# The MLP down projection in seven half-size products per unit, and two norms in one chain

## The reference, cut to what matters

```python
D_MODEL, SEQ, DEPTH, D_FF = 1024, 256, 2, 4096

def rmsnorm(x, g):
    y = x * lax.rsqrt(jnp.mean(x * x, axis=-1, keepdims=True) + EPS)
    return y * g

def squared_relu_mlp(h, w_up, w_down):
    return jnp.square(jax.nn.relu(h @ w_up)) @ w_down

def first_block(x, mem, ...):
    h = x
    for layer in range(DEPTH):
        h = h + mixer(rmsnorm(h, ...), ...)
        h = h + memory_cross_attention(rmsnorm(h, xa_norm[layer]), mem, ...)
        h = h + squared_relu_mlp(rmsnorm(h, mlp_norm[layer]), mlp_w_up[layer], mlp_w_down[layer])
    return rmsnorm(h, final_norm)

def second_block(x, c, ...):
    sh1, sc1, gt1, sh2, sc2, gt2 = split(silu(c) @ w_ada + b_ada)
    h = rmsnorm(x, norm1_w) * (1.0 + sc1) + sh1
    x = x + gt1 * hybrid_mixer(h, ...)
    h2 = rmsnorm(x, norm2_w) * (1.0 + sc2) + sh2
    return x + gt2 * expert_choice_ffn(h2, ...)
```

## Time and profile before

| | us |
|---|---|
| median of 3 runs | 1802.83 |
| lowest, highest | 1796.73, 1804.12 |
| profiled execution | 1800.43 |
| its span | 1798.6 |
| mean granted clock in it | 0.939 |
| TensorE busy, share of the span | 1567.6, 87% |
| VectorE busy | 450.9, 25% |
| ScalarE busy | 258.8, 14% |
| DMA, mean over the span | 220 GB/s |

### The profile page before, as it was taken

One profiled execution on the slowest core, in us unless ns is written; L12 is line 12 of the kernel. 1 busy time (PEld: TensorE's weight loads), 2 busy tenths in 40 slices (PEclk: granted clock), 3 DMA queues, 4 the chain that ended last, 5 costly groups with the idle time before them and its releaser, 6 DMA issues.

```text
span 1798.6 us, 20532 instructions
## 1 busy us (share of the span) xinstructions
PE 1567.6 (87%) x9012; PEld 1163.4 (65%) x9012; DVE 450.9 (25%) x1056; ACT 258.8 (14%) x606; POOL 30.3 (2%) x52
## 2 busy tenths in 40 slices
PE   5999999999999999999999899999977656566665
PEld 4867688888886777888888788768863212121212
DVE  3633015330033420253200355652330000000000
ACT  1232021000011510210000222232021000000000
POOL 0000000000010000000000002000000000000000
PEclk9999999999999999999999899998989888887778
DMA  9425316664443054157644101342549999999997
GB/s 383 148 93 187 140 47 234 240 266 154 153 158 140 1 187 152 47 222 272 250 166 143 47 1 48 117 134 102 246 175 388 429 429 429 429 430 429 429 428 316
DMA packets 42824, 395.25 MB, mean 220 GB/s; under 512 B 15856, under 2 KB 18288, under 8 KB 19056
## 3 DMA queue, kind: packets, MB, share of 16 engines
q1 hardware_dynamic: 42032, 392.46, 55.3%
q0 software_dynamic: 272, 1.05, 0.2%
q10 hardware_dynamic: 432, 0.44, 0.1%
HBM read 391.31 MB, written 2.62 MB: 219 GB/s over the span
## 4 chain that ended last, share of the span: by engine, by line
PE 74%; DMA 22%; DVE 2%; issue 1%; ACT 1%; ACTq 0%; DVEq 0%
PE pb L433 66%; DMA ring<-in_w_experts 22%; PE pb L521 6%; DMA small_w<-in_small_w 1%; PE pb L582 1%; PE pb L642 0%; DVE rstd L1616 0%; ACT arena L1274 0%; PE pb L1101 0%; PE pb L961 0%; PE pb L1108 0%; DVE xT L2152 0%; DVE arena L1676 0%; PE pb L727 0%; DVE sml L1703 0%
## 5 line engine op out<-in xcount | busy, mean ns | idle before, releaser
L433 PE MATMUL pb<-hT,ring 128*128 128x256 f32 x2176 | 483.2, 382 | 0.0
L433 PEld LDWEIGHTS pb<-hT,ring 128*128 128x128 f32 x2176 | 412.5, 191 | 62.9 <-issue 7.8
L433 PE MATMUL pb<-arena,ring 128*128 128x256 f32 (+3 forms) x1344 | 250.1, 353 | 3.1 <-DVE xT L1846 1.5
L433 PEld LDWEIGHTS pb<-arena,ring 128*128 128x128 f32 (+2 forms) x1344 | 219.5, 183 | 32.9 <-issue 5.0
L1274 ACT ACTIVATE arena<-pb 128x512 f32<-128x512 f32 (+4 forms) x166 | 77.9, 480 | 522.0 <-PE pb L433 429.8
L433 PE MATMUL pb<-ring,hT 128*32 128x512 f32 (+2 forms) x512 | 94.0, 657 | 36.9 <-DMA ring<-in_w_experts 36.9
L433 PE MATMUL pb<-arena 128*64 128x128 f32 (+5 forms) x592 | 96.7, 457 | 29.5 <-DMA arena<-in_w_experts 17.0
L521 PE MATMUL pb<-arena,ring 128*128 128x256 f32 x512 | 118.2, 382 | 0.0
L2140 DVE SCALAR_TENSOR_TENSOR side<-side,pb 128x256 f32<-128x256 f32 x16 | 6.7, 422 | 410.5 <-ACT side L1274 410.5
L521 PEld LDWEIGHTS pb<-arena,ring 128*128 128x128 f32 x512 | 94.9, 190 | 14.6 <-issue 2.9
L433 PE MATMUL pb<-ring,arena 128*32 128x512 f32 (+1 forms) x416 | 63.8, 720 | 45.4 <-DMA ring<-in_w_experts 45.4
(11 more groups left out here) (254 smaller groups left out, 1204.1 us busy)
## 6 DMA issues: line engine op xcount, KB each, us to landing
ring<-in_w_dense SPq DMA_DIRECT2D x86, 2048.0 KB, 8.0
ring<-in_w_experts SPq DMA_DIRECT2D x72, 2048.0 KB, 36.1
arena<-in_w_experts SPq DMA_DIRECT2D x24, 2048.0 KB, 36.0
ring<-in_w_dense SPq DMA_DIRECT2D x2, 1536.0 KB, 7.5
cons<-in_cons SPq DMA_DIRECT2D x1, 1808.0 KB, 19.6
xT<-in_xT SPq DMA_DIRECT2D x1, 1024.0 KB, 6.3
side<-in_memT POOLq DMA_DIRECT2D x1, 1024.0 KB, 6.3
out<-xT SPq DMA_DIRECT2D x4, 256.0 KB, 2.2
```

Of the source, the lines that this page charges most:

```text
L433: return nc.tensor.matmul(o, l, r, start=st, stop=sp)
```

## The change

Each unit of the down projection is a product of a 256x1024 block of hidden values and a 1024x512 block of weights. It is cut in halves along all three dimensions and computed as 7 products of half the size instead of 8, in Strassen's way. Four sums of weight quarters and four sums of hidden quarters are made by VectorE (`prepare`): three of the former go into spare memory and one in place into the ring slot; the latter go into `hT`. Now a chunk of 128 tokens is the stationary operand and 256 output features are the moving one. The 7 products collect over the four units of a side in the halves of four banks, 0 to 3 for side 0 and 4 to 7 for side 1. `collect` on VectorE, after a copy on ScalarE, makes the four quarters of the result from them; these have tokens on partitions, so TensorE transposes them (16 transposes per layer, 8 of them after unit 5 for side 0, and 8 after unit 7 for side 1) before VectorE adds them to `xT`.

The final norm and the next block's norm are made in one chain. ScalarE squares each chunk of `xT` twice, plain and scaled by `final_norm`; VectorE sums both over the chunks 0 to 6 (`add_both`); TensorE makes both means with 6 matmuls, the second with a term that accounts for EPS; VectorE scales `xT` directly into `hT` with the product of both gains (`gg`), and only then makes the final norm's `xT`.

The slots, sizes of loads and their order don't change. GpSimd waits for `pads` before it clears its workspace, whose memory the sums use. The core of the diff:

```diff
+        wsum = [view(arena, 10240, 4, S), view(arena, 11264, 4, S), view(arena, 12288, 3, S)]
+        hsum = [view(hTt, 512 * i, 4, P) for i in range(4)]
+        quarters = [more[:, S * i:S * (i + 1)] for i in range(4)]
...
-                for side_ in range(2):
-                    names = [f"dn{layer}_{side_}_{f}" for f in range(4)]
-                    banks = [fill(nm, f) for f, nm in enumerate(names)]
-                    for g in range(4):
-                        w, u = take()
+                for i in range(8):
+                    side_, g = divmod(i, 4)
+                    if g == 0:
+                        pq = [fill(f"pq{layer}_{side_}_{j}", 4 * side_ + j) for j in range(4)]
+                    w, u = take()
+                    down_unit[layer, i] = u
+                    h = hid[:, 8 * g:8 * g + 8, :]
+                    rows_ = {"11": lambda k: h[:, k, TOK[0]], "12": lambda k: h[:, 4 + k, TOK[0]], "22": lambda k: h[:, 4 + k, TOK[1]]}
+                    rows_ |= {f"s{j + 1}": lambda k, j=j: hsum[j][:, k, :] for j in range(4)}
+                    cols_ = {"11": lambda k: w[:, k, FEAT[0]], "21": lambda k: w[:, 4 + k, FEAT[0]], "22": lambda k: w[:, 4 + k, FEAT[1]],
+                             "t1": lambda k: wsum[0][:, k, :], "t2": lambda k: wsum[1][:, k, :], "t3": lambda k: w[:, k, FEAT[1]],
+                             "t4": wide_sum}
+                    step = 8 * (8 * layer + i)
+                    for n, (j, l, r, needs) in enumerate((((0, 0), "11", "11", 0), ((0, 1), "12", "21", 0), ((1, 1), "s1", "t1", 2),
+                                                          ((2, 0), "s2", "t2", 4), ((1, 0), "22", "t4", 5), ((2, 1), "s3", "t3", 7),
+                                                          ((3, 0), "s4", "22", 8))):
+                        if needs:
+                            pe.wait_ge(ws_ready, step + needs)
+                        for k in range(4):
+                            if side_ == 0 and n < 2 and k % 2 == 0:
+                                pe.wait_ge(hid_ready, 16 * layer + 4 * g + 2 * n + k // 2 + 1)
+                            last = nc.tensor.matmul(pq[j[0]][:, FEAT[j[1]]], rows_[l](k), cols_[r](k),
+                                                    start=g == 0 and k == 0 and n in (0, 2, 3, 6), stop=g == 3 and k == 3,
+                                                    skip_group_check=True)
+                        if n >= 2 or (n == 1 and g == 3):
+                            mark(last, f"pq{layer}_{side_}_{j[0]}", g == 3, u if n == 6 else None)
+                            product_done[layer, i, n] = (pq_bank := fillings[f"pq{layer}_{side_}_{j[0]}"][0], marks[pq_bank])
+                    if i == 0:
+                        modulation(6 * layer + 5)
+                    if i in (5, 7):
                         for f in range(4):
-                            for k in range(DC):
-                                if side_ == 0 and f == 0 and k % 2 == 0:
-                                    pe.wait_ge(hid_ready, 16 * layer + 4 * g + k // 2 + 1)
-                                last = mm(banks[f][:, 0:S], w[:, k, f * P:(f + 1) * P],
-                                          hid[:, 8 * g + k, :], g == 0 and k == 0, g == 3 and k == DC - 1)
-                            if g == 3 or f == 3:
-                                mark(last, names[f], g == 3, u if f == 3 else None)
-                        if side_ == 0 and g == 0:
-                            modulation(6 * layer + 5)
+                            ps = fill(f"dn{layer}_{i // 4 - (i == 5)}_{f}", f)
+                            for t in range(TT):
+                                pe.wait_ge(q_ready, 8 * layer + 4 * (i == 7) + (1, 2, 4, 3)[2 * (f // 2) + t])
+                                last = nc.tensor.transpose(ps[:, TOK[t]], quarters[2 * t + f // 2][:, (f % 2) * P:(f % 2 + 1) * P], ident)
+                            mark(last, f"dn{layer}_{i // 4 - (i == 5)}_{f}")
...
-            norm("final")
-            norm("n1")
+            sums = [fill("norm_final"), fill("norm_n1")]
+            pe.wait_ge(sum_ready, SUMMED.index("final") + 1)
+            mm(sums[0][:, 0:S], ones, sq[:, 0, :], True, False)
+            mm(sums[1][:, 0:S], ones, raw(0), True, False)
+            mm(sums[1][:, 0:S], epsm, sq[:, 0, :], False, False)
+            pe.wait_ge(norm_sq, 8 * NORMS.index("final") + 16)
+            mm(sums[1][:, 0:S], ones, raw(7), False, False)
+            mark(mm(sums[1][:, 0:S], epsm, sq[:, 7, :], False, True), "norm_n1")
+            mark(mm(sums[0][:, 0:S], ones, sq[:, 7, :], False, True), "norm_final")
...
+                for i in range(2):
+                    if i:
+                        copied(act, *(f"dn{layer}_0_{f}" for f in range(4)))
+                    ps, _ = full(act, f"pq{layer}_{i}_0")
+                    fn(quarters[0], ps[:, FEAT[0]], ACT.Copy).then_inc(q_copied, 1)
+                    for c in range(4 * i, 4 * i + 4):
+                        copied(act, f"dn{layer}_{c // 4}_{c % 4}")
+                        if layer == 0:
+                            fn(sq[:, c, :], xT[:, c, :], ACT.Square).then_inc(norm_sq, 1)
+                        else:
+                            fn(sq[:, c, :], xT[:, c, :], ACT.Square)
+                            fn(raw(c), xT[:, c, :], ACT.Square, scale=col("final_norm", c)).then_inc(norm_sq, 2)
...
-            squares(xT, [f"dn1_{c // 4}_{c % 4}" for c in range(DC)])
-            root("final")
-            squares(xT, signal=fin_ready)
-            root("n1")
+            ps, free = full(act, "norm_n1")
+            fn(rt[:, :], ps[:, 0:S], ACT.Sqrt, scale=1.0 / D, bias=eps2).then_inc(free, 1)
+            ps, free = full(act, "norm_final")
+            fn(raw(1), ps[:, 0:S], ACT.Sqrt, scale=1.0 / D, bias=eps).then_inc(free, 1)
...
+                prepare(layer, 0)
+                prepare(layer, 1)
                 modulated(6 * layer + 4)
                 modulated(6 * layer + 5)
+                if layer:
+                    copied(dve, *(f"ada{i}" for i in range(12)))
+                    link(V.scalar_tensor_tensor(g1s, modc[:, 8:16], 1.0, col("norm1", 0, 8), ALU.add, ALU.mult))
+                    V.tensor_tensor(gg, g1s, col("final_norm", 0, 8), ALU.mult)
+                prepare(layer, 2)
+                prepare(layer, 3)
+                prepare(layer, 4)
+                collect(layer, 0)
+                prepare(layer, 5)
+                prepare(layer, 6)
                 for c in range(DC):
+                    if c == 4:
+                        prepare(layer, 7)
+                        collect(layer, 1)
                     name = f"dn{layer}_{c // 4}_{c % 4}"
                     ps, free = full(dve, name)
                     V.tensor_tensor(xT[:, c, :], xT[:, c, :], ps[:, 0:S], ALU.add).then_inc(free, 1)
...
                         V.tensor_scalar(raw(c), xT[:, c, :], gain(c), None, ALU.mult).then_inc(raw_ready, 1)
                         if c > 1:
                             add_square(c - 1)
+                    elif c > 1:
+                        add_both(c - 1)
...
+            def prepare(layer, i):
+                u, g = down_unit[layer, i], i % 4
+                w, h = slot_ap(u), hid[:, 8 * g:8 * g + 8, :]
+                step = 8 * (8 * layer + i)
+                def used(n):
+                    if i:
+                        b, m = product_done[layer, i - 1, n]
+                        dve.wait_ge(filled[b], m)
+                def combine(o, x, y, op, last=True):
+                    ins = V.tensor_tensor(o, x, y, op)
+                    if last:
+                        ins.then_inc(ws_ready, 1)
+                if i == 0:
+                    dve.wait_ge(hid_ready, 16 * (layer + 1))
+                dve.wait_ge(loaded[slot_of[u]], 16 * nth[u])
+                w11, w12, w21, w22 = (w[:, HALF[a_], FEAT[b_]] for a_ in range(2) for b_ in range(2))
+                h11, h12, h21, h22 = (h[:, HALF[b_], TOK[a_]] for a_ in range(2) for b_ in range(2))
+                used(2)
+                combine(wsum[0], w12, w11, ALU.subtract)
+                combine(hsum[0], h21, h22, ALU.add)
+                used(3)
+                dve.wait_ge(ws_ready, step + 2)
+                combine(wsum[1], w22, wsum[0], ALU.subtract)
+                combine(hsum[1], hsum[0], h11, ALU.subtract)
+                used(4)
+                dve.wait_ge(ws_ready, step + 4)
+                combine(wsum[2], wsum[1][:, 0:3, :], w21[:, 0:3, :], ALU.subtract, False)
+                combine(wide_sum(3), wsum[1][:, 3, :], w21[:, 3, :], ALU.subtract)
+                used(5)
+                combine(hsum[2], h11, h21, ALU.subtract)
+                combine(w12, w22, w12, ALU.subtract)
+                used(6)
+                combine(hsum[3], h12, hsum[1], ALU.subtract)
+            def collect(layer, i):
+                banks = [fillings[f"pq{layer}_{i}_{j}"][0] for j in range(4)]
+                ps = [pb[:, b, :] for b in banks]
```

(59 more changed lines are left out.)

## The result

The changed kernel takes 1794.35 us (median of 5, 1789.16 to 1796.51) against 1801.08 (median of 5) for the kernel before: ratio 0.9945, interval 0.9925 to 0.9965. The gain is 7 us between the medians and 10 by the ratio, where 23 were forecast. The time lies above the range of 1770 to 1789. The first long expert transfer begins at 1358.10 us, 11.4 earlier than before (1369.49), where 23 were forecast too.

The account below looks back on a forecast made before the run. TensorE was taken as the bound up to 1369.5 us, before a train of expert transfers that moves with it. Layer 0's -9.6 and layer 1's -13.8 made -23.4 us, 1777.0 profiled and 1779 median, range 1770 to 1789.

Parts of the forecast that it names:

- First unit: Start of each layer's down projection: TensorE stalls for VectorE's first sums, 0.45 us per layer with the wake-up.
- the sum: Whole kernel: layer 0 -9.6 and layer 1 -13.8, together -23.4 us, giving a median of 1779; chance 0.63.
- I put the steady state at no stall: Down projection units after the first: VectorE's sums run nearly a unit ahead, so TensorE never waits for them.
- A: Stretch from layer 0's up projection to where the next projection waits for its last chunk; layer 0 forecast -9.6 us.
- B: Stretch from layer 1's up projection to the next block's first matmul; layer 1 forecast -13.8 us.
- The banks: Between the down projection's sides: side 1 no longer waits for side 0's banks, -1.5 us in all.
- The end of layer 0: Last product to the next projection's eighth matmul: 5.7 us where it was 3.0, so +2.7 us.
- The end of layer 1: Last product to the next block's first matmul: 14.3 us instead of 15.9, low clock included, a gain of 1.6.
- The gain reached the end: Expert transfers after the layers: the rival said they don't start earlier and time stays at 1803; chance 0.05.
- eight transposes: Turning the result back, after units 5 and 7: 1.9 us per eight; those after unit 5 add 1.9 per layer.
- the clock rival: Clock falls after unit 5 in both layers and at layer 0's end: three falls of 1.7 us, 1784.5; chance 0.20.
- VectorE did not become the bound: Each unit: the rival had VectorE's sums taking twice the rows' time, 15.7 us a unit, ending at 1836; chance 0.05.

Follow-up runs that it names:

- e1: Changed kernel, but VectorE reads the fifth modulation sum before the sums of units 0 and 1: 1782.01 us, ratio 0.9884 to the kernel before.
- e3: Changed kernel with each layer's sixth modulation in bank 5 instead of bank 4, VectorE's order unchanged: 1770.14 us, one run.
- e9: Changed kernel plus 8 unused matmuls where TensorE waits after unit 0, VectorE's order unchanged: 1784.55 us, ratio 0.9886 to the kernel before.
- e8: Changed kernel with each layer's sixth modulation in bank 5 instead of 4, timed over 4 runs: 1777.25 us, ratio 0.988 to the kernel before.
- e5: Changed kernel with the fifth modulation sum read earlier, plus three more 128x1024 VectorE sums in each of units 2 to 6: 1777.62 us, one run.
- e6: Changed kernel with the fifth modulation sum read earlier, plus eight more 128x1024 VectorE sums in each of units 2 to 6: 1822.23 us, one run.
- e4: Changed kernel with the fifth modulation sum read earlier, and each transpose after unit 5 made six times: 1783.96 us, one run.
- e7: Changed kernel with the fifth modulation sum read earlier, plus 8 and 5 unused matmuls in layer 1's end gaps: 1767.16 us, ratio 0.9829 to the kernel before.

## Why the prediction was wrong

**The step that failed** is the part *First unit*, and with it the sum, which has no term for what the new sums are queued in front of. It asks only when the sums are ready for TensorE (0.45 us per layer, which came true). Of VectorE's queue it says: "three modulation steps, from 391.54 to 393.86; only then come the sums". But `modulated(4)` and `modulated(5)` stood on VectorE directly behind the last modulation step, and the change puts the sums of units 0 and 1 before them; this was put at nothing without a reason. The first of the two frees the bank that TensorE needs after unit 0. The fence of the diff shows the new order, and the kernel's line `fill(f"ada{i}", 4)` the bank. Before, that read began at 393.77, at once, and cost nothing. "I put the steady state at no stall" did hold: from 420 to 497 us the changed kernel's TensorE has no wait. The missing term: 4.06 us of waiting and 3.0 us of low clock behind it, per layer, 14.0 us in all; e1 and e3 take it away by two independent edits, and e9's trace splits it. With it the forecast of -23.4 becomes -9.4, where the stretches gave -11.5 and both timings, by their ratio, -9.9.

Without that wait the kernel is where the forecast said: 1782 and 1777 in e1 and e8, inside the range around 1779. Stretch by stretch in e1: A -10.5 (forecast -9.6), B -15.0 (forecast -13.8). Each is about 1 us better than forecast, mostly by the transposes (below); the first long expert transfer comes 19.4 us earlier in e1's profile and 26.7 in e8's, around the 23 of the forecast.

**Right**: the unit, 12.08 us for 12.10. VectorE's sums, 1.22 us for 1.227 and some 7.5 a unit for 7.8, and room for 11.1 us of work per unit (e5), not for 17.2 (e6). The stall in the first unit: products with sums begin 0.2 and 0.25 us late, 0.45 as forecast. The banks: the gap between the sides is gone. The end of layer 0: from 497.81 to 503.47, 5.66 us for 5.7. The end of layer 1: 14.4 for 14.3, the low clock during the sums included, though by some luck: the chunks' sums were ready 6.3 us after the last product and not 6.7, and from the first matmul on them to the root it took 4.6 us and not 4.0. The final norm moved behind cost nothing that the traces show: VectorE takes up its next job at 1004.13 in the changed kernel, 7.2 us after the block's first matmul, as before. The gain reached the end: without the wait the timings are 20 us below the kernel before.

**Mis-sized**: eight transposes take 0.88 us and not 1.9. The earlier trace rows were read as three transposes of two instructions each; six instructions there are six transposes (two heads of three), and a float32 transpose is one instruction of 109 ns. That is 2 us in the kernel's favour. Not seen: the up projection's last bank is freed 0.35 us later in layer 0 (idle 0.76 in place of 0.41 us).

**The rivals**: the clock rival had a price that fits (1.7 to 5.1 us a fall; 3.0 measured) and the wrong places. The clock fell at none of the three seams that it named, but at a fourth that it didn't, behind a wait. VectorE did not become the bound by the length of its sums; it held TensorE up by their order.

## What to carry to other kernels

When work is put into an engine's queue, read what stands behind the insertion, not only whether the new work fits: a read of 0.15 us that frees a bank was delayed by 15 us and cost more than half of a 23 us gain. A wait of 4 us on TensorE cost 7 here, because the clock fell behind it, so a hole is priced with the slow stretch after it. Where a gap couldn't be closed, unused matmuls into a free half bank kept the clock up and paid for themselves: 2.8 us per layer behind the wait in e9, 2.0 us at the end of layer 1 in e7, both by the traces.

## What was not expected of the hardware

- Forty-eight float32 transposes in a row, 5.2 us of nothing else, left the granted clock at 1.00 (e4).
- While sixteen matmuls of 32 columns ran (32 instructions, TensorE shown as busy all the while), it fell to 0.50, although dense matmuls and only 0.8 us of idling stood before them; it rose again during the wide matmuls behind (e7). No run separates what in this stretch did it.
- VectorE reading and writing weights in the ring at 94% busy, beside dense matmuls that read the same units, changed neither engine's instruction times (e5).
